# Moving the second layer's modulation out of the prelude and onto GpSimd, inside the first three delta heads

## The chip, the cores and the metric

The kernel runs on one core of one Trainium2 chip. The metric is device time in microseconds (us) for one execution, as the median of several runs. In the profile the engines are called PE (TensorE), DVE (VectorE), ACT (ScalarE), POOL (GpSimd) and SP (SyncE, which only issues DMAs here). SBUF is the on-chip memory that all engines reach, PSUM the one in which TensorE adds up.

## The reference

Two blocks run one behind the other on 256 tokens (the first also on 256 context tokens), all in float32. The part that matters here is the first block: two layers, each of which begins with a modulation, a shift, a scale and a gate per channel, worked out from one conditioning vector for the latent tokens and one for the context.

```python
sc_lat, sc_ctx = jax.nn.silu(c), jax.nn.silu(c_ctx)
for i in range(DEPTH):                     # DEPTH = 2
    shift, scale, gate = jnp.split(sc_lat @ ada_w[i] + ada_b[i], 3, axis=-1)
    shift_c, scale_c, gate_c = jnp.split(sc_ctx @ ada_w[i] + ada_b[i], 3, axis=-1)
    u_lat = rms_norm(h_lat, norm_g[i]) * (1.0 + scale[:, None]) + shift[:, None]
    u_ctx = rms_norm(h_ctx, norm_g[i]) * (1.0 + scale_c) + shift_c
    ...     # layer 0: gated delta rule, 8 key heads; layer 1: attention
```

ada_w[i] is 1024 x 3072 float32, 12.6 MB for each layer. The second layer's modulation depends on c and c_ctx alone, and nothing needs it before the first layer has ended.

## The kernel before

The kernel is a row of stages. In each stage every engine has its own list of instructions, and semaphores tie them together; `Chain` (`link` in the code) makes an engine wait for each of its own instructions before the next. Weights come through a ring, `w_ring`: two sets of slots of 512 KB, filled by SP in groups (`Stream.in_stage`). SP fills a set when TensorE has used what lay in it.

The **prelude** is the first stage. It runs over 12 groups of four weight chunks, six for each layer. For a group, TensorE multiplies the two columns silu(c) with 512 columns of weights (`row_sums`, L505), VectorE copies the sums to SBUF (`row_out`, L588), TensorE turns them so that channels lie on partitions (`turn`, L517), and VectorE adds the bias (`add`, L593). The first layer's six groups are mixed with the norm of h and the gates of the delta rule, whose last pieces are exponentials on ScalarE (L578 to L580) and copies into `sc` on VectorE (`put`, L485). Four of the second layer's groups come after them.

Then a short stage clears two buffers on GpSimd (L752, L753) while VectorE casts and copies some constants (L760 to L763). A stage with the front of head 0 follows, and then one long stage with **eight heads** (`QK_HEADS`, numbered from 0). In head n, TensorE inverts the triangular matrices by levels and then goes through four scan steps. Between these it runs the projections of head n+1 in small portions (`front.products`, L798). VectorE does the masks, differences and states of head n, and between them the convolution of head n+1: one `conv` is L824 and four times L826, and after it comes a `silu`, L832. In step 1 of the scan it does one conv, in steps 2 and 3 one silu and one conv each. At the end of a head GpSimd takes two inverse roots (`inverse_root`, L148: first `rc` for head n+1's norms, then `ms` for head n's output) and scales the output, L1000. TensorE spreads `rc` over partitions (L162), and VectorE scales q and k by it (L860), convolves the last part and builds the next head's matrices (L905). What has to come after what on an engine is the order of the code; there is no scheduler.

SP waits, before it loads the ring's next group of six chunks, until the first head's six projections are done (`summed`, once per head).

Of the kernel before, what the change touches and what calls it, by code (L numbers as in the profile page):

```python
# [21 lines left out]
P = 128  # L22
D = 1024
KT = D // P
# [141 lines left out]
class Sets:  # L166
# [3 lines left out]
    SIZE = 56  # L170
# [296 lines left out]
def prelude(nc, st, bank, C, h, h_loaded, c_cols, g_cols, biases, mods, rows, pick, silu_c, sq, rs, gs, u, w_ab, dt_rows, a_rows, sc,  # L467
# [6 lines left out]
    count, per_layer = 12, 6  # L474
    streams = ((0, CTX, 1), (CTX, SEQ, 0))
    mod = mods[0]
# [13 lines left out]
    with stage(nc, names) as (s, block):  # L490
# [7 lines left out]
        def _(pe):  # L498
# [45 lines left out]
            row_sums(6)  # L544
# [38 lines left out]
        def _(dve):  # L583
# [6 lines left out]
            def add(g):  # L590
                layer, at = g // per_layer, 4 * (g % per_layer)
                dve.wait_ge(s["turned"], g + 1)
                link(nc.vector.tensor_tensor(mods[layer][:, at:at + 4, :], bank[2 + g % 2][:, 0:8].rearrange("p (j c) -> p j c", c=2),  # L593
                                             biases[layer][:, at:at + 4].unsqueeze(2).to_broadcast([P, 4, 2]), ALU.add), s["added"])
# [51 lines left out]
            row_out(6)  # L646
# [10 lines left out]
            row_out(7)  # L657
            add(6)
# [17 lines left out]
def delta_heads(nc, st, bank, banks, C, CS, u, sc, conv_cols, o_cols, gated, spare):  # L676
# [8 lines left out]
    with ExitStack() as es:  # L685
# [49 lines left out]
        short = es.enter_context(nc.sbuf_tensor("short", [P, 3 * P], mybir.dt.bfloat16))  # L735
        th = y
# [176 lines left out]
        with stage(nc, front_names) as (s, block):  # L913
# [46 lines left out]
            def _(dve):  # L960
# [13 lines left out]
                for c in range(4):  # L974
# [5 lines left out]
                 "o_sum o_sqd o_mean o_root o_norm o_turned o_out ")  # L980
        st.begin(DN_GROUP)
        with stage(nc, names + front_names) as (s, block):
            fronts = [Front(s, zs_of[(n + 1) % 2], hs_of[(n + 1) % 2], n) for n in range(QK_HEADS - 1)]
            st.in_stage(QK_HEADS - 1, DN_GROUP, s["proj"], block)
# [7 lines left out]

            def pool_head(pool, link, n):
# [10 lines left out]
            def tensor_head(pe, n):  # L1004
# [145 lines left out]
                if more:  # L1150
# [10 lines left out]
                    ahead(REST)  # L1161
                    pe.wait_ge(s["kq_done"], front.up("kq_done", 2))
# [83 lines left out]
            def vector_head(dve, link, n):  # L1246
# [77 lines left out]
                if more:  # L1324
# [5 lines left out]
                    output(1)  # L1330
                    front.chain(dve, link, 2)
# [300 lines left out]
def flat(a):  # L1632

    return a.rearrange("p a b -> p (a b)")
# [1157 lines left out]
def build(nc, a, out, col_at):  # L2792

    with ExitStack() as top:
# [36 lines left out]
        with ExitStack() as es:  # L2831
# [5 lines left out]
            with ExitStack() as l0:  # L2837
                sc = sb("sc", [P, QK_HEADS, PER_HEAD], l0)
                o_cols = sb("o_cols", [P, 1], l0)
                with ExitStack() as e3:  # L2840
# [5 lines left out]
                    sc_t = sb("silu_c", [P, KT, 2], e3)  # L2846
# [603 lines left out]
```

## Time and profile before

| | us |
|---|---|
| median of 3 runs (2161.9 to 2168.11) | 2164.07 |
| the profiled execution's own time | 2163.62 |
| its span, first to last instruction | 2161.8 |
| TensorE busy in the span | 1962.7 |
| VectorE busy | 1031.1 |
| ScalarE busy | 595.1 |
| GpSimd busy | 74.1 |

The span is shorter than the time by what lies around the instructions. TensorE's busy time is modelled and includes overlaps, so a share near 100% in a stretch means that it hardly waits there. The profile's granted clock is TensorE's, as a share of 2.4 GHz; its mean is 0.955.

### The profile page before, as it was taken

How to read it: one execution, taken by the hardware profiler on the slowest of the kernel's cores; microseconds unless marked ns; L12 is line 12 of the kernel's file. 1: busy time of each engine (PE TensorE's matmuls, PEld its weight loads, DVE VectorE, ACT ScalarE, POOL GpSimd, SP SyncE). 2: the span in 40 equal slices, each digit the busy share in tenths (PEclk: the TensorE clock that was granted, in tenths of full speed). 3: DMA queues.
4: the chain of work that ended last, by engine and by line, in shares of the span. 5: the costliest groups of instructions: out<-in, count | busy, mean ns of one | idle time of the engine just before them, and what ended most of it. 6: DMA issues, size and time to landing. Idle time of an engine off the chain costs nothing. (4 is left out here: it accounts for less than half of the span.)

```text
span 2161.8 us, 40136 instructions
## 1 busy us (share of the span) xinstructions
PE 1962.7 (91%) x16700; PEld 1438.4 (67%) x16700; DVE 1031.1 (48%) x2064; ACT 595.1 (28%) x1275; POOL 74.1 (3%) x50
## 2 busy tenths in 40 slices
PE   5789999999999999789798889988989899989998
PEld 2346666666666666544376777767776798878887
DVE  3346756675766767411114457775455543311101
ACT  1023434444343434400203324232332321000000
POOL 0000101000010101000000000000000000000000
PEclk8899999999999999889899989989999999999999
DMA  8801001010101010022131243231012122434443
GB/s 326 303 31 61 35 26 60 2 60 1 60 1 61 1 61 1 2 117 78 44 117 40 78 169 117 91 119 46 32 60 89 60 78 79 175 117 156 155 176 136
DMA packets 52240, 184.73 MB, mean 85 GB/s; under 512 B 5856, under 2 KB 9312, under 8 KB 51552
## 3 DMA queue, kind: packets, MB, share of 16 engines
q1 hardware_dynamic: 52064, 182.23, 22.5%
q8 instruction: 130, 2.13, 0.4%
q14 instruction: 46, 0.38, 0.1%
HBM read 180.11 MB, written 2.10 MB: 84 GB/s over the span
## 5 line engine op out<-in xcount | busy, mean ns | idle before, releaser
L798 PE MATMUL banks<-u,w_ring 128*128 128x512 f32 x768 | 356.7, 600 | 6.4 <-PEq L195 6.4
L386 PE MATMUL banks<-u,w_ring 128*128 128x256 f32 x1056 | 251.4, 390 | 8.4 <-PEq L195 8.4
L798 PEld LDWEIGHTS banks<-u,w_ring 128*128 128x128 f32 x768 | 140.5, 192 | 133.2 <-issue 130.1
L386 PEld LDWEIGHTS banks<-u,w_ring 128*128 128x128 f32 x1056 | 200.1, 196 | 42.6 <-issue 17.4
L410 PE MATMUL banks<-u,w_ring 128*128 128x256 f32 x704 | 153.7, 382 | 4.8 <-PEq L195 4.8
L410 PEld LDWEIGHTS banks<-u,w_ring 128*128 128x128 f32 x704 | 134.8, 192 | 23.6 <-issue 5.0
L3229 PE MATMUL banks<-gated,w_ring 128*128 128x512 f32 (+1 forms) x384 | 140.9, 530 | 2.8 <-PEq L195 2.8
L3229 PEld LDWEIGHTS banks<-gated,w_ring 128*128 128x128 f32 x384 | 73.9, 193 | 69.4 <-issue 66.2
L826 DVE SCALAR_TENSOR_TENSOR acc<-raw,hc,acc 128x512 f32<-128x512 f32 x128 | 96.2, 752 | 4.5
L3229 PE MATMUL banks<-ffn,w_ring 128*128 128x256 f32 x352 | 77.9, 385 | 3.0 <-PEq L195 3.0
L1195 ACT ACTIVATE acc<-banks 128x512 f32<-128x512 f32 x80 | 47.8, 597 | 105.4 <-PE banks L1060 105.2
L3229 PEld LDWEIGHTS banks<-ffn,w_ring 128*128 128x128 f32 x352 | 68.0, 194 | 12.8 <-issue 3.4
L3084 DVE SCALAR_TENSOR_TENSOR ffn_tanh<-ffn_tanh,banks 128x256 f32<-128x256 f32 x22 | 9.2, 417 | 136.7 <-ACT ffn_tanh L3076 136.7
L1272 DVE TENSOR_TENSOR y<-banks,const_base 128x512 f32<-128x512 f32 x80 | 55.3, 691 | 34.8 <-PE banks L1049 33.6
L1049 PE MATMUL banks<-acc,a_t 64*64 64x64 f32 x2560 | 60.2, 232 | 11.9 <-issue 7.4
L1276 DVE TENSOR_TENSOR acc<-acc,banks 128x512 f32<-128x512 f32 x80 | 55.1, 688 | 33.2 <-PE banks L1076 31.6
L441 PE MATMUL banks<-u,w_ring 128*128 128x256 f32 (+1 forms) x192 | 57.5, 462 | 12.8 <-PEq L195 12.8
L1076 PE MATMUL banks<-y,acc 64*64 64x64 f32 x2560 | 57.9, 228 | 12.2 <-ACT acc L1195 5.5
L3123 ACT ACTIVATE tail_sq<-h 128x256 f32<-128x256 f32 (+1 forms) x28 | 13.2, 470 | 194.3 <-DVE h L2871 91.7
L1049 PEld LDWEIGHTS banks<-acc,a_t 64*64 64x64 f32 x2560 | 48.4, 141 | 25.3 <-issue 16.2
L1076 PEld LDWEIGHTS banks<-y,acc 64*64 64x64 f32 x2560 | 47.5, 137 | 24.4 <-issue 19.3
L1218 ACT ACTIVATE dec<-banks,hs 128x128 f32<-128x128 f32 x128 | 47.1, 368 | 57.2 <-PE banks L1133 53.8
(490 smaller groups left out, 3141.9 us busy)
## 6 DMA issues: line engine op xcount, KB each, us to landing
w_ring<-in_w SPq DMA_DIRECT2D x321, 512.0 KB, 6.2
h<-in_h SPq DMA_DIRECT2D x2, 2048.0 KB, 10.0
const_base<-in_const SPq DMA_DIRECT2D x1, 1216.0 KB, 5.5
hold<-h SPq DMA_DIRECT2D x1, 1024.0 KB, 5.5
const_part<-in_const SPq DMA_DIRECT2D x1, 1024.0 KB, 4.9
h<-hold SPq DMA_DIRECT2D x1, 1024.0 KB, 9.4
out<-u SPq DMA_DIRECT2D x8, 128.0 KB, 1.9
const_part<-in_const SPq DMA_DIRECT2D x1, 640.0 KB, 4.5
```

The costliest lines, as they stand in the source:

```text
L386: mm = self.nc.tensor.matmul(place, self.st.chunk(g % 2, slot)[:, P * k:P * k + P], self.src(k), start=(k == 0), stop=(k == KT - 1))
L410: last = nc.tensor.matmul(out, lhs[k], rhs[k], start=(k == 0), stop=(k == n - 1))
L441: mm = nc.tensor.matmul(bank[q % banks][:, 0:n_tok], st.chunk(h, c)[:, P * b:P * b + P], src(k), start=(k == 0), stop=(k == k_tiles - 1))
L798: mm = nc.tensor.matmul(self.places[m % len(self.places)][:, :], (st.slot(m) if g is None else st.chunk(g % 2, m))[:, P * k:P * k + P], u[ ...
L826: link(nc.vector.scalar_tensor_tensor(out, raw[:, m, :, i:i + SEQ], hc[:, 5 * m + i:5 * m + i + 1], out, ALU.mult, ALU.add), self.s["conv" ...
L1049: mm = nc.tensor.matmul(block_of(bank[2 * d + hb], t, j), a_block(2 * j + d, t, hb, hb), inv[half(hb), d, 2 * t + j, :], start=True, stop= ...
L1076: mm = nc.tensor.matmul(block_of(bank[2 * d + j], t, hb), invt_c[half(j), d, 2 * t + hb, :], prod[half(j), d, hb, t, :], start=True, stop= ...
L1195: link(nc.scalar.activation(invt_c[:, d].rearrange("p s e -> p (s e)"), bank[4 + d][:, :], ACT.Copy), s["t_out"])
L1218: link(nc.scalar.activation(tile(vn[:, d, :], j), tile(bank[2], 2 * d + j), ACT.Copy, scale=col(BETA, 2 * j + d, t)), s["vn_ready"] if j a ...
L1272: link(nc.vector.tensor_tensor(prod[:, d], both(sums(2 * d, 256)), mask(d, lv), ALU.mult), s["p_ready"])
L1276: link(nc.vector.tensor_tensor(by_chain(inv[:, d]), by_chain(inv[:, d]), both(sums(2 * d, 256)), ALU.subtract), s["t_ready"])
L3229: mm = nc.tensor.matmul(bank[m % banks][:, 0:n], st.chunk(g % 2, c)[:, P * (at % 8):P * (at % 8) + P], src(k), start=(k == 0), stop=(k == ...
```

## The change

The second layer's six groups go out of the prelude: 24 chunks less in the ring, six fewer `row_sums`, `row_out`, `turn` and `add`. The same weights are now an input of their own (`mods`, 24 chunks of 128 x 1024). SP loads them in heads 0, 1 and 2, eight for each head, behind the ring's group of that head, into two buffers in `gated` (whose slots for later heads are still free). GpSimd multiplies each chunk with silu(c), once for each of the two streams, and adds the products up in four accumulators (`modulation`), ahead of the two roots of that head. TensorE sums the accumulators over the partitions with 16 one-column products (`modulation_sums`), and VectorE adds the bias (`modulation_out`). The code, cut to its core:

```diff
-def prelude(nc, st, bank, C, h, h_loaded, c_cols, g_cols, biases, mods, rows, pick, silu_c, sq, rs, gs, u, w_ab, dt_rows, a_rows, sc,
+def prelude(nc, st, bank, C, h, h_loaded, c_cols, g_cols, bias, mod, rows, pick, silu_c, sq, rs, gs, u, w_ab, dt_rows, a_rows, sc,
-    count, per_layer = 12, 6
+    count = 6
...
             row_sums(5)
             turn(4)
-            row_sums(6)
             turn(5)
...
             nc.tensor.matmul(bank[4][:, 0:P], C("ones"), lg, start=True, stop=True).then_inc(s["sums"], 1)
-            for g in range(7, count):
-                row_sums(g)
-                turn(g - 1)
-            turn(count - 1)
...
             link(nc.vector.tensor_tensor(gx, lg, bank[4][:, 0:128], ALU.add), s["ex"])
-            row_out(7)
-            add(6)
             dve.wait_ge(s["e_ready"], 4)
...
-            for g in range(8, count):
-                row_out(g)
-                add(g - 1)
-            add(count - 1)
...
+        MOD_HEADS, MOD_CHUNKS = 3, 8
+        w_of = [flat(gated[:, 6 + 2 * i:8 + 2 * i, :]) for i in range(2)]
+        w_part = flat(gated[:, 10:12, :])
+        mod_acc = [[gated[:, 12 + 2 * i + c, :] for c in range(2)] for i in range(2)]
...
+            def mods_in(sp, n, lo, hi):
+                for i in range(lo, hi):
+                    q = MOD_CHUNKS * n + i
+                    if q >= 2:
+                        sp.wait_ge(s["w_used"], q - 1)
+                    sp.dma_start(w_of[q % 2], mod_w[q]).then_inc(s["w_in_odd" if q % 2 else "w_in_even"], 16)
...
-            st.in_stage(QK_HEADS - 1, DN_GROUP, s["proj"], block)
+            st.in_stage(QK_HEADS - 1, DN_GROUP, s["proj"], block, None, {n: all_in(n) for n in range(MOD_HEADS)})
...
+            def modulation(pool, link, n):
+                if n:
+                    pool.wait_ge(s["mod_summed"], n)
+                for i in range(MOD_CHUNKS):
+                    q, at = MOD_CHUNKS * n + i, 2 * (i % 4)
+                    w = w_of[q % 2].rearrange("p (j e) -> p j e", j=2)
+                    pool.wait_ge(s["w_in_odd" if q % 2 else "w_in_even"], 16 * (q // 2) + 16)
+                    for c in range(2):
+                        out = mod_acc[i // 4][c]
+                        link(nc.gpsimd.tensor_tensor(w_part.rearrange("p (j e) -> p j e", j=2), w,
+                                                     silu_c[:, at:at + 2, c:c + 1].to_broadcast([P, 2, 512]), ALU.mult),
+                             s["w_used"] if c else None)
+                        if at:
+                            link(nc.gpsimd.tensor_tensor(out, out, w_part[:, 0:512], ALU.add))
+                        link(nc.gpsimd.tensor_tensor(out, out if at else w_part[:, 0:512], w_part[:, 512:1024], ALU.add),
+                             s["mod_added"] if c and i == MOD_CHUNKS - 1 else None)
...
+            def modulation_sums(pe, n):
+                pe.wait_ge(s["mod_added"], n + 1)
+                for i in range(2):
+                    for c in range(2):
+                        for j in range(4):
+                            col = 8 + 8 * i + 2 * j + c
+                            mm = nc.tensor.matmul(bank[2][:, col:col + 1], tile(mod_acc[i][c], j), C("ones")[:, 0:1],
+                                                  start=True, stop=True)
+                mm.then_inc(s["mod_summed"], 1)
...
             def pool_head(pool, link, n):
...
+                if n < MOD_HEADS:
+                    modulation(pool, link, n)
                 if more:
                     front.root(pool)
...
                     front.grams(pe)
                     ahead(REST)
+                    if n < MOD_HEADS:
+                        modulation_sums(pe, n)
...
                     output(1)
+                    if n < MOD_HEADS:
+                        modulation_out(dve, link, n)
```

What it moves on SP, in the stage with the eight heads (`w_ring<-in_w` is a chunk of the ring, `gated<-in_mods` one of the second layer's modulation):

```order
 L297 UNCONDITIONAL_BRANCH
-L215 DMA w_ring<-in_w 128x1024 x36
+L215 DMA w_ring<-in_w 128x1024 x6
+L986 DMA gated<-in_mods 128x1024 x8
+L215 DMA w_ring<-in_w 128x1024 x6
+L986 DMA gated<-in_mods 128x1024 x8
+L215 DMA w_ring<-in_w 128x1024 x6
+L986 DMA gated<-in_mods 128x1024 x8
+L215 DMA w_ring<-in_w 128x1024 x18
```

Eight loads now stand behind the ring's group of heads 0, 1 and 2 each; each of them but the first two waits until a buffer is free.

On GpSimd, from the start of head 0 in the same stage, before the change (`rc` and `ms` are the two roots, `h` the scaling):

```order
L148 TENSOR_TENSOR rc<-rc,const_base 128x8
L148 TENSOR_TENSOR ms<-ms,const_base 128x8
L1000 TENSOR_TENSOR h<-h,ms 128x1024
L148 TENSOR_TENSOR rc<-rc,const_base 128x8
L148 TENSOR_TENSOR ms<-ms,const_base 128x8
```

and the last pieces of head 0's modulation with what follows, in the changed kernel (L1008 is the product of a chunk, L1012 and L1013 the additions):

```order
L1008 TENSOR_TENSOR gated<-gated,silu_c 128x1024
L1012 TENSOR_TENSOR gated<-gated 128x512
L1013 TENSOR_TENSOR gated<-gated 128x512
L148 TENSOR_TENSOR rc<-rc,const_base 128x8
L148 TENSOR_TENSOR ms<-ms,const_base 128x8
L1040 TENSOR_TENSOR h<-h,ms 128x1024
L1008 TENSOR_TENSOR gated<-gated,silu_c 128x1024
L1013 TENSOR_TENSOR gated<-gated 128x512
```

In heads 0 to 2, 16 products and 28 additions now stand ahead of the roots of the head on this engine.

On TensorE, at the end of head 0 of the changed kernel, from the second of the two Gram products (L866) to the turning of the output (L1210):

```order
L866 MATMUL banks<-qn,kn 128x128 x4
L794 MATMUL banks<-u,w_ring 128x512 x2
L1022 MATMUL banks<-const_base,gated 128x1 x16
L1210 MATMUL banks<-const_base,h 128x128 x8
L881 MATMUL banks<-short 128x512
```

The 16 one-column products, L1022, are new; the rest stood there in this order.

## Rows read from the trace of the kernel before

**Rows 1.** Busy time by stretch, head 1: length, then each engine's busy us.
```profile
core 0: us, PE busy (x) PEld busy (x) DVE busy (x) ACT busy (x) POOL busy (x), PEclk, DMA share, GB/s
...
258.00:355.00 97.00, 93.58 (x1116) 63.48 (x1115) 65.03 (x115) 41.30 (x91) 6.14 (x3) 1.00 0.09 34
```

**Rows 2.** Timeline, the prelude's end: start, duration, engine, line, [idle before].
```profile
69.79 0.28 ACT L580 ACTIVATE gate_tmp<-banks 128x128 f32<-128x128 f32 x1
...
70.53 0.96 DVE L485 COPY sc<-gate_tmp 128x64 f32<-128x64 f32 x4
...
72.12 0.97 DVE L485 COPY sc<-gate_tmp 128x64 f32<-128x64 f32 x4
...
92.81 0.17 DVE L593 TENSOR_TENSOR mod<-banks,cols 128x8 f32<-128x8 f32 x1 [0.77 <-PE banks L517]
```

**Rows 3.** Timeline, the short stage behind the prelude.
```profile
93.54 1.83 POOL L752 MEMSET raw<- 128x2080 f32 x1 [62.45 <-POOLq L195]
93.58 1.87 DVE L760 CAST short<-const_base 128x128 bf16<-128x128 f32 x1 [0.60 <-DVE mod L593]
95.31 1.88 POOL L753 MEMSET inv_t<- 128x2048 f32 x1
95.48 2.05 DVE L760 CAST short<-const_first 128x128 bf16<-128x128 f32 x2
```

**Rows 4.** Timeline, the end of head 1, GpSimd and VectorE.
```profile
337.71 1.23 DVE L1318 TENSOR_TENSOR h<-h 128x1024 f32<-128x1024 f32 x1
337.82 2.61 POOL L148 TENSOR_TENSOR rc<-rc,const_base 128x8 f32<-128x8 f32 x1 [89.70 <-DVE rc L846]
...
341.76 1.63 POOL L148 TENSOR_TENSOR ms<-ms,const_base 128x8 f32<-128x8 f32 x1 [1.33 <-DVE ms L1323]
...
343.47 1.90 POOL L1000 TENSOR_TENSOR h<-h,ms 128x1024 f32<-128x1024 f32 x1
...
343.57 0.69 DVE L860 SCALAR_TENSOR_TENSOR qn<-y,banks 128x512 f32<-128x512 f32 x1
...
344.29 1.36 DVE L824 TENSOR_SCALAR acc<-raw,hc 128x512 f32<-128x512 f32 x1
```

**Rows 5.** Timeline of VectorE in head 1, the scan.
```profile
293.42 0.69 DVE L1284 TENSOR_TENSOR h<-gram_kq,rn 128x512 f32<-128x512 f32 x1
...
298.23 0.43 DVE L1308 COPY state<-banks 128x256 f32<-128x256 f32 x1 [2.39 <-PE banks L1146]
...
304.68 0.49 DVE L824 TENSOR_SCALAR acc<-raw,hc 128x512 f32<-128x512 f32 x1
305.20 3.11 DVE L826 SCALAR_TENSOR_TENSOR acc<-raw,hc,acc 128x512 f32<-128x512 f32 x4
310.47 0.73 DVE L1312 SCALAR_TENSOR_TENSOR state<-state,hs,banks 128x128 f32<-128x128 f32 x2 [2.16 <-PE banks L1146]
...
312.46 0.42 DVE L1315 TENSOR_TENSOR h<-banks,rn 128x256 f32<-128x256 f32 x1
...
322.71 0.73 DVE L1312 SCALAR_TENSOR_TENSOR state<-state,hs,banks 128x128 f32<-128x128 f32 x2 [1.45 <-PE banks L1146]
...
335.36 0.88 DVE L1315 TENSOR_TENSOR h<-banks,rn 128x256 f32<-128x256 f32 x2 [1.85 <-PE banks L1143]
337.51 0.17 DVE L846 TENSOR_SCALAR rc<-banks 128x8 f32<-128x8 f32 x1 [1.26 <-PE banks L155]
```

**Rows 6.** Timeline of TensorE in head 1, three places.
```profile
314.66 0.59 PE L1123 MATMUL banks<-state,kn 128*128 128x256 f32 x2
...
335.55 1.84 PE L155 MATMUL banks<-const_base,gram_kq 128*128 128x1 f32 x16
...
342.13 1.04 PE L162 MATMUL banks<-const_base,rc 128*128 128x128 f32 x8
```

**Rows 7.** Timeline of SP's DMA queue, the groups loaded in heads 0 and 1.
```profile
162.04 2.72 SPq L215 DMA_DIRECT2D w_ring<-in_w  x6
...
263.51 2.80 SPq L215 DMA_DIRECT2D w_ring<-in_w  x6
```

**Rows 8.** DMA issues from 93 to 300 us: size, median us from issue to landing.
```profile
w_ring<-in_w SPq DMA_DIRECT2D x20, 512.0 KB, 7.1
```

More of the change, by code:

```diff
@@ L166 @@
 class Sets:
-    SIZE = 56
+    SIZE = 60
     FIRST = 116
@@ L590, in add @@
             def add(g):
-                layer, at = g // per_layer, 4 * (g % per_layer)
+                at = 4 * g
                 dve.wait_ge(s["turned"], g + 1)
-                link(nc.vector.tensor_tensor(mods[layer][:, at:at + 4, :], bank[2 + g % 2][:, 0:8].rearrange("p (j c) -> p j c", c=2),
-                                             biases[layer][:, at:at + 4].unsqueeze(2).to_broadcast([P, 4, 2]), ALU.add), s["added"])
+                link(nc.vector.tensor_tensor(mod[:, at:at + 4, :], bank[2 + g % 2][:, 0:8].rearrange("p (j c) -> p j c", c=2),
+                                             bias[:, at:at + 4].unsqueeze(2).to_broadcast([P, 4, 2]), ALU.add), s["added"])
             for n in range(2):
@@ L667, in _, with delta_heads @@
                 link(put(BEND, x, d))
-            for g in range(8, count):
-                row_out(g)
-                add(g - 1)
-            add(count - 1)
     st.passed(count, 4)
-def delta_heads(nc, st, bank, banks, C, CS, u, sc, conv_cols, o_cols, gated, spare):
+def delta_heads(nc, st, bank, banks, C, CS, u, sc, conv_cols, o_cols, gated, spare, nxt):
     order = ((0, 1, 2, 3), (1, 0, 3, 2))
@@ L991, in head, with modulation_out @@
                         fronts[n - 1] if n else None, lambda name, count: COUNTS[name] * n + count)
+            def modulation(pool, link, n):
[23 more added lines that the diff above has]
+                mm.then_inc(s["mod_summed"], 1)
+            def modulation_out(dve, link, n):
+                dve.wait_ge(s["mod_summed"], n + 1)
+                link(nc.vector.tensor_tensor(mod_next[:, 8 * n:8 * n + 8, :], bank[2][:, 8:24].rearrange("p (j c) -> p j c", c=2),
+                                             mod_bias[:, 8 * n:8 * n + 8].unsqueeze(2).to_broadcast([P, 8, 2]), ALU.add))
             def pool_head(pool, link, n):
@@ L2854, in build @@
                     finish_loads(nc, loads, small)
-                    prelude(nc, st, bank, C, h, late, cc("c"), cc("norm_g", 0, 8), [cc("ada_b", 24 * i, 24 * i + 24) for i in range(2)],
-                            mods, rows, pick, sc_t, sq, rs, gs, u, w_ab, gate_rows[:, 0, :], gate_rows[:, 1, :], sc, tmp,
+                    prelude(nc, st, bank, C, h, late, cc("c"), cc("norm_g", 0, 8), cc("ada_b", 0, 24),
+                            mods[0], rows, pick, sc_t, sq, rs, gs, u, w_ab, gate_rows[:, 0, :], gate_rows[:, 1, :], sc, tmp,
                             cc("dn_o"), o_cols[:, :])
@@ L2859, in build @@
                 mod = mods[0]
-                delta_heads(nc, st, bank, banks, C, CS, u, sc, cc("conv"), o_cols[:, 0:1], gated, h)
+                delta_heads(nc, st, bank, banks, C, CS, u, sc, cc("conv"), o_cols[:, 0:1], gated, h, (a["mods"], sc_t, mods[1], cc("ada_b", 24, 48)))
                 start_loads(nc, [(h[:, :, :], a["h"].rearrange("p (k t) -> p k t", k=KT))], late)
@@ L3371, in layout @@
     att = f("att_w_in")[0]
-    stream = [row_chunks(ada[0]), row_chunks(ada[1]), fm(np.concatenate(heads, axis=1)), fm_tiles(f("dn_w_out")[0]),
+    stream = [row_chunks(ada[0]), fm(np.concatenate(heads, axis=1)), fm_tiles(f("dn_w_out")[0]),
               fm(att[:, 1024:1536]), fm(att[:, 0:1024]), fm(att[:, 1536:2560]), fm(f("att_w_out")[0])]
```

10 lines of the change are left out of this document (6 added, 4 removed).

## Prediction

> **What bounds the kernel now.** I read the stretches first, then the two places that the change touches. In a head TensorE is busy for 93.58 of 97 us at full clock and VectorE for 65 [rows 1]: the heads run at TensorE's pace, and VectorE has gaps that depend on where in the head it is. The timeline of the prelude's end shows something else. ScalarE's last exponential ends at 70.07, VectorE's last copies into `sc` at 73.09, and then 20 us pass with nothing but the second layer's modulation, up to 92.98 [rows 2]. The next stage waits for that end and begins at 93.54 [rows 3].
>
> **What goes.** Without `row_out(7)` and `add(6)` ahead of them the copies start at 70.1 instead of 70.53, so the prelude ends at about 92.98 - 20.3 = 72.7: **20.3 us less**. The row before, `row_out(6)`, lay in a wait and gives nothing. The ring holds head 0's first chunks by then, since SP ordered them when group 4 was summed. What follows moves as a block. Bounds: 19 and 21.
>
> **GpSimd's work.** Nearest row for a product: L1000, 128 x 1024 with a broadcast input, 1.90 us; the gap between linked instructions is 0.08 (341.76 + 1.63 to 343.47) [rows 4]. No row shows a 128 x 512 addition on GpSimd; half of L1000 is 0.95, the whole of it 1.90, and I take 0.98, since the form is the same and only the fixed part isn't halved. A head: 16 x 1.90 + 28 x 0.98 + 44 x 0.08 = **61.3 us**, mean instruction 1.31. The chunks come behind six of the ring: SP issues those from 263.51 to 266.31 in head 1 [rows 7], and a chunk lands 7.1 us after its issue [rows 8], so GpSimd starts at about 274 (in this trace's time) and, alone, ends at 335.3. Behind it on GpSimd waits `rc`'s root, wanted at 337.8 [rows 4]. In head 0 it starts at about 172.5, some 4 us earlier in the head.
>
> **Do the two engines hinder each other?** The rows say so. VectorE's first cast started at 93.58, took 1.87 and ended 0.08 behind GpSimd's memset; the next one got in only behind the second memset [rows 3]. So an instruction waits for the whole of the other's, and they take turns. The same at the end of a head: L824 takes 0.49 alone, but beside L1000 it took 1.36 and ended 0.28 behind it [rows 4, 5]. The root takes 1.63 alone and 2.61 beside L1318, which reads two SBUF tensors [rows 4]. L860, with one SBUF tensor and one in PSUM, took 0.69 beside L1000, as without it [rows 4]. What no row shows is a VectorE instruction with two SBUF tensors, L826, held up by a long GpSimd instruction. Its price lies between 0 and a whole GpSimd instruction. I take the turns of [rows 3], because L1318 shows that this kind uses what GpSimd needs.
>
> The Trainium skill (SBUF — State Buffer, Who interferes with whom) has this as a rule: "A DVE instruction with two SBUF inputs contends with a GpSimd instruction that reads SBUF", and the one that starts second is blocked until the other is done. By it the sum below stands at 2165; by the rows of casts and L824 alone, only L824 and small copies would pay, and the sum would be 2147.
>
> **The cost in a head.** Of an instruction of VectorE 0.49 - 0.27 = 0.22 us is hidden behind the other's [rows 4, 5], so a turn costs 1.31 - 0.22 = 1.09, the first of a run half an instruction, 0.7.
> - L1284, two small copies and L1299: 4.0 us more. VectorE waits 2.39 for TensorE right behind them [rows 5], and TensorE reaches the result about as much later. Nothing.
> - Step 1, a conv: 0.7 + 4 x 1.09 = 5.1. Cover: VectorE's wait of 2.16, and TensorE takes the state at 314.66 although it is there at 312.88, 1.78 [rows 5, 6]. Left: 1.1.
> - Step 2, silu and conv: 6.1, cover 1.45 + 1.78. Left: 2.9.
> - Step 3: 6.1, cover 1.85 + 1.26 [rows 5]. Left: 3.0.
>
> So `rc`'s mean (L846) is 7.0 late, at 344.5. GpSimd is itself held up by some 20 instructions for 0.45 each or less, about 8 us, and ends at 335.3 + 8 = 343.4: just ahead of it, so the root isn't late for GpSimd's sake. The spread on TensorE had 1.7 to spare (340.43 to 342.13), but `ms` and L1000 are 7.0 late and hold up the last conv: **6.6** a head. In head 0 the modulation ends 4 us earlier, and step 3 pays a third: **4.7**. Together 4.7 + 6.6 + 6.6 = **17.9 us**.
>
> **The small parts.** 16 one-column products took 1.84 us [rows 6]. They stand where VectorE is full; turning the output, and with it ScalarE's last decays, comes later, by about 1.2 us a head: **3.5** with VectorE's addition (0.17 each), bounds 0 and 5.5. The cover is TensorE's lead there; if it is gone, 5.5. The moved DMAs, 24 of 512 KB, fall into a stretch where the engines of the DMA are 9% busy [rows 1]; SP blocks on them until GpSimd is nearly through, but its next group is wanted only a head later.
>
> **Sum**: 2163.62 - 20.3 + 17.9 + 3.5 = 2164.7, say **2165**. The profiled time lies within 0.5 us of the median, so it stands for both.
>
> **Rivals.**
> 1. *No hold-up for two SBUF tensors* (20%). For it: no row shows it. Against: L1318 and the root. Then 2163.6 - 20.3 + 3.5 = 2147.
> 2. *Hold-up at half the price* (12%): VectorE gets two instructions in per turn, or the covers are larger. Runs of 3 and 3.5 instead of 5.1 and 6.1 stay within their covers, only the last leaves some: some 2 us a head, 2153. Faster too.
> 3. *GpSimd becomes the bound* (25%). The margin to the root is 344.5 - 343.4, 1.1 us. If an addition takes 1.15 instead of 0.98, a head's modulation is 4.8 us longer; the root starts 3.7 later in heads 1 and 2, and every turn costs 0.11 more, over 17 turns 1.9. That is 4 to 6 a head, 2165 + 13 = 2178. It decides from a mean instruction of 1.34. Slower than before.
> 4. *One SBUF tensor is enough* (5%): L1293, L1312 and L1315, some 25 a head, pay as well: 20 us a head, 2220. Against: L860.
>
> The Trainium skill (GPSIMD Engine Reference, Elementwise — side-by-side cycle accounting) bears on rival 3: it gives 4497 ns for a 2048-element addition, an estimate of 1.12 us for 512 and 2.25 for 1024. L1000's 1.90 is lower than that, and the row decides for the product; with 1.12 for the additions alone the estimate would be about 2176.
>
> **How the numbers follow.** My forecast has 38%; its own range, with the bounds of the small parts and of the covers, is 2158 to 2171. 0.3% (6.5 us) is about what a measurement tells from no change. Faster: rivals 1 and 2, 0.32. Same: the forecast, 0.38. Slower: rivals 3 and 4, 0.30. The range goes from 2146, rival 1, to 2181, rival 3; it leaves out the lower part of 1, the upper part of 3, and 4.
>
> **What would show it.** Right: the prelude's last VectorE instruction at about 72.7; L1008 at 1.9 us and L1012 at 0.98; in heads 0 to 2 the four L826 of a conv spread over 8 us instead of 3.1, each ending about 0.6 behind a GpSimd instruction; levels ahead of the scan unchanged; heads 3 to 6 unchanged; three heads longer by 6 to 8 us. If L826 stays at 0.75 in the first three heads, rival 1 holds. If the root starts right behind L1013 and long after L846, it is rival 3. If L1315 or L1293 are stretched, it is rival 4. Wrong from the start would be a prelude that ends later than 74, or a first product of head 0 that waits for its chunk.

## The result, and the profile after

The changed kernel takes 2197.53 us (median of 4 runs, 2193.54 to 2207.41), the kernel before 2165.63 us (median of 4, 2161.9 to 2168.11). The ratio is 1.0169, 95% interval 1.0148 to 1.0191: 32 us slower, where "no change" was forecast with 2146 to 2181 as the range. The profiled execution is the one of 2207.41 us, span 2205.7; its prelude ran at a lower clock than that of most other kernels below, and I come back to it.

The timeline of the prelude in the changed kernel, and where the next stage begins [rows 3]:

```profile
50.14 13.92 PE L538 MATMUL banks<-w_ab,u 128*128 128x64 f32 x64
...
83.50 1.83 POOL L748 MEMSET raw<- 128x2080 f32 x1 [51.74 <-POOLq L195]
```

The memset that stood at 93.54 stands at 83.50: 10 us earlier, not 20. The 64 products of L538 take 13.92 us; the line is L539 in the kernel before. The granted clock of this stretch is half:

```profile
50.00:64.00 14.00, 14.00 (x69) 13.74 (x70) 0.69 (x1) 1.37 (x3) 0.00 (x0) 0.50 0.55 218
```

The columns are those of [rows 1]; the third number from the end is the clock, 0.50, that is 1.2 GHz. Now GpSimd in head 1 (start, duration, engine), with SP's queue above it:

```profile
271.57 2.79 SPq L215 DMA_DIRECT2D w_ring<-in_w  x6
274.40 62.09 SPq L986 DMA_DIRECT2D gated<-in_mods  x8
```

```profile
284.18 1.89 POOL L1008 TENSOR_TENSOR gated<-gated,silu_c 128x1024 f32<-128x1024 f32 x1 [34.84 <-DMA gated<-in_mods]
286.15 1.27 POOL L1013 TENSOR_TENSOR gated<-gated 128x512 f32<-128x512 f32 x1
...
355.97 2.22 POOL L1008 TENSOR_TENSOR gated<-gated,silu_c 128x1024 f32<-128x1024 f32 x1
...
359.61 1.26 POOL L1013 TENSOR_TENSOR gated<-gated 128x512 f32<-128x512 f32 x1
360.95 1.65 POOL L148 TENSOR_TENSOR rc<-rc,const_base 128x8 f32<-128x8 f32 x1
```

A product takes the 1.89 us that were expected. An addition takes 1.27, not 0.98. A head's modulation lasts from 284.18 to 360.87, 76.7 us, and `rc`'s root starts right behind it. VectorE in the same head, the scan [rows 5] and what follows:

```profile
310.43 1.51 DVE L1335 SCALAR_TENSOR_TENSOR rn<-banks,hs,v_t 128x128 f32<-128x128 f32 x4 [2.23 <-PE banks L1163]
311.98 1.08 DVE L820 TENSOR_SCALAR acc<-raw,hc 128x512 f32<-128x512 f32 x1
313.09 7.28 DVE L822 SCALAR_TENSOR_TENSOR acc<-raw,hc,acc 128x512 f32<-128x512 f32 x4
...
325.23 2.10 DVE L828 SCALAR_TENSOR_TENSOR y<-y,acc 128x512 f32<-128x512 f32 x1
327.37 1.38 DVE L820 TENSOR_SCALAR acc<-raw,hc 128x512 f32<-128x512 f32 x1
328.78 7.91 DVE L822 SCALAR_TENSOR_TENSOR acc<-raw,hc,acc 128x512 f32<-128x512 f32 x4
...
344.47 7.92 DVE L822 SCALAR_TENSOR_TENSOR acc<-raw,hc,acc 128x512 f32<-128x512 f32 x4
...
353.34 0.17 DVE L842 TENSOR_SCALAR rc<-banks 128x8 f32<-128x8 f32 x1
...
363.94 0.69 DVE L856 SCALAR_TENSOR_TENSOR kn<-y,banks 128x512 f32<-128x512 f32 x1 [5.72 <-PE banks L162]
...
376.22 0.75 DVE L1295 SCALAR_TENSOR_TENSOR gated<-banks,o_cols,zs 128x512 f32<-128x512 f32 x1 [4.96 <-PE banks L1210]
```

The four L822 of a conv (L826 before) take 7.3 to 7.9 us instead of 3.11, while L1335, with one SBUF tensor, still takes 1.51 for four. The mean (L842) starts at 353.34 and the root at 360.95, 7.6 us behind it, where it was 0.3 before [rows 4, 5]: the root waits for GpSimd. Then VectorE waits twice, 5.72 us for the spread of the root and 4.96 for the turned output. TensorE in that place:

```profile
362.74 1.94 PE L162 MATMUL banks<-const_base,rc 128*128 128x128 f32 x8 [6.35 <-POOL rc L148]
...
370.99 4.17 PE L1022 MATMUL banks<-const_base,gated 128*128 128x1 f32 x32
375.02 1.95 PE L1210 MATMUL banks<-const_base,h 128*128 128x128 f32 x8
...
377.19 1.92 PE L885 MATMUL banks<-const_base,hs 128*128 128x128 f32 x8
```

Three things are to be seen: it stood idle for the root, its spread then took 1.94 where it took 1.04 [rows 6], and the sixteen sums are 32 instructions and 4.17 us. (The `order` view ahead of the prediction lists the program's products, x16; a trace lists instructions, x32.)

Since the prelude's clock differs from execution to execution, I compare the heads by a length that leaves it out: from the start of `rc`'s root in the stage ahead of head 0 to that of head 5, read from GpSimd's timeline. It is 128.9 to 734.6 before and 119.9 to 778.7 after: 605.7 and 658.8 us. So heads 0 to 5 lost 53.0 us in this execution and the prelude gave 9.0 back; the spans differ by 43.9, so on balance nothing is to be explained behind the heads. The experiments are given with this length too, as "the heads".

Each head can be cut in three, at the starts of the root, of the scan's first L1335 and of `rc`'s mean: what lies behind the root of the head before, with the levels; the scan; and the wait of the root, from the mean to the root. Before, the scan takes 34.4 us and the wait 0.2 to 0.3 in each of the six heads. The last three columns, read from the profiled executions, give the difference to before, summed over heads 0 to 5. The columns of the scan and of the root are steady: kernels in which GpSimd has no modulation work stay within 0.2 of before. The column behind the root is not: the kernel with the modulation left out runs the same heads as the kernel before and differs by 3.6, so a few us there, and in the length of the heads, tell nothing.

| kernel | median us | ratio to before | the heads, us | behind the root | scan | root late |
|---|---|---|---|---|---|---|
| before | 2165.63 | | 605.7 | | | |
| changed | 2197.53 | 1.0169 | 658.8 | 10.9 | 23.0 | 19.1 |
| modulation left out | 2141.88 | 0.9912 | 602.0 | -3.6 | -0.2 | 0.0 |
| sums only | 2154.48 | 0.9963 | 606.7 | 1.0 | -0.1 | 0.0 |
| sums only, in two halves | 2147.94 | 0.9937 | 605.3 | -0.4 | -0.1 | 0.0 |
| write-only GpSimd | 2162.6 | 0.9997 | 619.5 | 2.0 | -0.2 | 11.9 |
| products only, early | 2152.66 | 0.9954 | 613.7 | 7.4 | 0.5 | 0.1 |
| products only, late | 2188.59 | 1.0113 | 649.6 | 9.8 | 34.0 | 0.1 |
| wide additions | 2191.22 | 1.0135 | 652.1 | 9.8 | 36.5 | 0.1 |
| sums later | 2197.06 | 1.0151 | 658.6 | 7.7 | 26.1 | 19.1 |
| five heads | 2171.11 | 1.0036 | 630.1 | 10.1 | 9.7 | 4.5 |
| even chunks | 2160.95 | 0.9998 | 621.8 | 8.1 | 8.0 | 0.1 |
| even and early | 2156.2 | 0.9968 | 614.5 | 4.5 | 4.3 | 0.1 |

Each ratio is to runs of the kernel before on the same chip; their medians are 2165.63 beside the changed kernel and 2161.14 to 2163.15 beside the others.

### The profile page after: what moved, and what is told of

The parts are those of the page before. It is cut to its first block and busy times, and to the rows that moved or that the text cites. A ratio compares the mean times of both kernels' runs of the same rounds, so it can differ in the third digit from the quotient of the medians.

```text
span 2205.7 us, 40172 instructions
## 1 busy us (share of the span) xinstructions
PE 1977.3 (90%) x16652; PEld 1460.1 (66%) x16652; DVE 1090.5 (49%) x2055; ACT 594.5 (27%) x1275; POOL 292.1 (13%) x182
## 5 line engine op out<-in xcount | busy, mean ns | idle before, releaser
L794 PE MATMUL banks<-u,w_ring 128*128 128x512 f32 x768 | 364.3, 611 | 13.3 <-PEq L195 13.3
L822 DVE SCALAR_TENSOR_TENSOR acc<-raw,hc,acc 128x512 f32<-128x512 f32 x128 | 136.3, 1065 | 4.5
L1008 POOL TENSOR_TENSOR gated<-gated,silu_c 128x1024 f32<-128x1024 f32 x48 | 97.4, 2030 | 119.9 <-DMA gated<-in_mods 116.4
L148 POOL TENSOR_TENSOR rc<-rc,const_base 128x8 f32<-128x8 f32 x8 | 17.0, 2126 | 405.0 <-DVE rc L842 404.8
L1013 POOL TENSOR_TENSOR gated<-gated 128x512 f32<-128x512 f32 x48 | 69.9, 1457 | 3.8
L441 PE MATMUL banks<-u,w_ring 128*128 128x256 f32 (+1 forms) x192 | 57.7, 463 | 12.8 <-PEq L195 12.8
```

Of the source, the lines that this page charges most:

```text
L441: mm = nc.tensor.matmul(bank[q % banks][:, 0:n_tok], st.chunk(h, c)[:, P * b:P * b + P], src(k), start=(k == 0), stop=(k == k_tiles - 1))
L794: mm = nc.tensor.matmul(self.places[m % len(self.places)][:, :], (st.slot(m) if g is None else st.chunk(g % 2, m))[:, P * k:P * k + P], u[ ...
L822: link(nc.vector.scalar_tensor_tensor(out, raw[:, m, :, i:i + SEQ], hc[:, 5 * m + i:5 * m + i + 1], out, ALU.mult, ALU.add), self.s["conv" ...
L1008: link(nc.gpsimd.tensor_tensor(w_part.rearrange("p (j e) -> p j e", j=2), w, silu_c[:, at:at + 2, c:c + 1].to_broadcast([P, 2, 512]), ALU. ...
L1013: link(nc.gpsimd.tensor_tensor(out, out if at else w_part[:, 0:512], w_part[:, 512:1024], ALU.add), s["mod_added"] if c and i == MOD_CHUNK ...
```

## The experiments

My theory after the result: the prelude's gain is whole, and the heads lose it through turns with GpSimd (whose price depends on what of VectorE's work they lie beside), through GpSimd's own length, and through the sums. The rivals: that the products' number alone sets the price, that the moved DMAs or GpSimd's mere activity do, or that the prelude gave only 10.

### The modulation left out

No part of the second layer's modulation is computed; the layer takes the first layer's values.

```
-            st.in_stage(..., {n: all_in(n) for n in range(MOD_HEADS)})
+            st.in_stage(...)
...
-                if n < MOD_HEADS:
-                    modulation(pool, link, n)
```

> The second layer's modulation is left out altogether (its values are a copy of the first layer's): no loads, no GpSimd work, no one-column products. What is left of the change is the shorter prelude. Theory A, the prelude's end moves by its idle tail: 20 us less than before, 2144. Theory B, TensorE's clock takes part of it back, since the work ahead of the end no longer keeps it up (in the changed kernel's trace the first stage ended only 10 us earlier, and head 0 began 7 earlier): 7 to 12 us less, 2153 to 2157.

2141.88 us, ratio 0.9912 (0.9886 to 0.9939): 20.7 us less than before, for the 20.3 of the forecast, as theory A had it. Its prelude:

```profile
47.45 7.36 PE L538 MATMUL banks<-w_ab,u 128*128 128x64 f32 x64
...
73.58 1.83 POOL L748 MEMSET raw<- 128x2080 f32 x1 [42.99 <-POOLq L195]
```

The memset is 20.0 earlier than before, with L538 at full clock. So the prelude gives what was forecast. The clock of L538 is at half in three of the thirteen profiled executions: the changed kernel's, that of five heads and that of even and early. In these three L538 starts later (49.28 to 50.14) than in any of the other ten (46.68 to 49.10), and the clock stands at 0.50 over the 3 us from 47 to 50, where the others show 0.67 to 1.00. Why it doesn't rise there was not tested. It costs some 9 us where it happens; the kernel with the sums later, which does the same prelude as the changed one at full clock, has its memset at 73.58 too.

### The sums only

GpSimd clears the accumulators once, TensorE sums those zeros in heads 0 to 2, VectorE adds the bias; the products and additions are left out, and so are the chunks' DMAs.

```
+                nc.gpsimd.memset(flat(gated[:, 12:16, :]), 0.0).then_inc(s["padded"], 1)
...
-                pe.wait_ge(s["mod_added"], n + 1)
...
-                    modulation(pool, link, n)
```

> As the run before, but with TensorE's 16 one-column products and VectorE's addition in heads 0 to 2, on accumulators that are cleared once (the loads and GpSimd's products and additions are left out). Theory A, the sums cost 1.2 us a head, as predicted: 3.5 us over the kernel without them. Theory B, they are 32 instructions of TensorE and take 3.75 us a head where VectorE waits for the output's turning: 8 to 11 us over the kernel without them.

2154.48 us, 0.9963 (0.9946 to 0.998), on theory B's side: 12.6 more than without, with ten runs from 2147.33 to 2157.98. The spans of the two profiled executions differ by 9.3: 3.0 ahead of the heads' length, 4.7 in it and 1.7 behind it. Of the 3.0, 1.6 come from this experiment's own clearing of the accumulators, beside which two casts of VectorE take 3.61 us instead of 2.05; they aren't a cost of the sums. From head 0's root to head 3's, the stretch that holds the sums, it is 303.5 us, and 295.1 with none: 8.4. TensorE's timeline and its granted clock in head 1:

```profile
330.38 3.63 PE L1022 MATMUL banks<-const_base,gated 128*128 128x1 f32 x32
...
335.02 1.91 PE L886 MATMUL banks<-const_base,hs 128*128 128x128 f32 x8
```

```profile
330.00:334.00 4.00, 4.00 (x35) 3.76 (x34) 2.32 (x6) 0.00 (x0) 0.00 (x0) 1.00 0.00 0
335.00:338.00 3.00, 3.00 (x14) 2.82 (x13) 2.69 (x7) 0.89 (x3) 0.00 (x0) 0.50 0.00 0
```

32 one-column instructions in a row, then half clock: eight transposes in 1.91 us that take 1.05 at full. It doesn't always come. In head 0 of the same execution the clock stays full:

```profile
230.92 3.63 PE L1022 MATMUL banks<-const_base,gated 128*128 128x1 f32 x32
...
235.53 1.05 PE L886 MATMUL banks<-const_base,hs 128*128 128x128 f32 x8
```

Over the traces of the changed kernel and the experiments there are 22 such rows of 32; what follows is slowed in 19 and not in 3.

### GpSimd that only writes

Each product and each addition is replaced by a memset of about its duration (the values are not computed). The memsets are a little shorter (1.80 and 1.23 us, against 1.89 and 1.27). The DMAs, their waits and the sums stay.

```
-                        link(nc.gpsimd.tensor_tensor(w_part..., w, silu_c..., ALU.mult), ...)
+                        link(nc.gpsimd.memset(mod_clear[:, 0:2048], 0.0), ...)
...
-                            link(nc.gpsimd.tensor_tensor(out, out, w_part[:, 0:512], ALU.add))
+                            link(nc.gpsimd.memset(mod_clear[:, 0:1360], 0.0))
```

> GpSimd's products and additions are replaced by as many memsets of about the same length (1.88 and 1.27 us), which write SBUF and read nothing; the modulation's values are zero plus bias. The loads, the waits, the order and the sums stay. Theory A (turns with VectorE's two-tensor instructions because GpSimd reads): L822 goes back to 0.75 us; GpSimd still holds the root back by its own length, since 69 us from its start end some 8 us behind the root's time; so the heads are 8 to 10 us longer than before instead of 19, and the kernel about 30 us faster than the changed one. Theory B (any GpSimd instruction holds up any VectorE instruction with two SBUF tensors): L822 stays near 1.8 us and the time stays at 2195.

2162.6 us, 0.9997 (0.9977 to 1.0017): 35 us less than the changed kernel, 39.3 in the heads, and theory A holds. In head 1, GpSimd first, VectorE's convs behind it:

```profile
266.48 1.81 POOL L1007 MEMSET gated<- 128x2048 f32 x1 [34.89 <-DMA gated<-in_mods]
```

```profile
295.24 3.11 DVE L823 SCALAR_TENSOR_TENSOR acc<-raw,hc,acc 128x512 f32<-128x512 f32 x4
...
319.47 1.99 DVE L821 TENSOR_SCALAR acc<-raw,hc 128x512 f32<-128x512 f32 x1
```

L823 is back at 3.11 with GpSimd at work all through the scan, for 66.3 us in this head. This is the largest part of the loss: GpSimd's reading. The Trainium skill (SBUF — State Buffer, Who interferes with whom) says that a VectorE instruction with two SBUF inputs contends with a GpSimd instruction that reads SBUF and not with one that only writes; the trace agrees, 7.28 beside reads and 3.11 beside writes. L821, with one input, took 0.49 alone and 1.99 here: some instructions are held up by writes too. But that costs nothing here: the scan's column is back at that of the kernel before. The heads are still 12.8 longer than with the sums only, and 11.9 of that is the root, which starts 5.8 us behind the mean in head 1. That is the price of GpSimd's length alone.

### Wide additions

Three of four pairs of 128 x 512 additions become one of 128 x 1024: the same elements, fewer and longer instructions.

```
-                            link(nc.gpsimd.tensor_tensor(out, out, w_part[:, 0:512], ALU.add))
-                        link(nc.gpsimd.tensor_tensor(out, ..., w_part[:, 512:1024], ALU.add), ...)
+                            link(nc.gpsimd.tensor_tensor(wide, wide, w_part, ALU.add))
```

> The products are added up over 1024 columns at once and folded to 512 once a group: 12 additions of 1024 and 4 of 512 a head instead of 28 of 512. All of the reference is computed. Alone, GpSimd then needs 61 us a head instead of 70. Theory A (GpSimd's length decides, the root waits for it): 9 us less in each of three heads, 25 us less than the changed kernel, about 2170. Theory B (VectorE's waits in the convolutions decide): each turn is longer, 1.9 us instead of 1.5, so nothing is won or 5 to 10 us lost.

2191.22 us, 1.0135 (1.0107 to 1.0162). GpSimd in heads 1 and 2, and the root of head 1:

```profile
L1014 POOL TENSOR_TENSOR gated<-gated 128x1024 f32<-128x1024 f32 x24 | 60.5, 2522 | 1.9
```

```profile
351.63 2.62 POOL L148 TENSOR_TENSOR rc<-rc,const_base 128x8 f32<-128x8 f32 x1 [4.23 <-DVE rc L843]
```

GpSimd is idle for 4.23 us ahead of the root: it is no longer late. Yet only 6.3 us came back, since each turn is now with a longer instruction: a conv's four L823 take 9.00 and 10.06 us in steps 1 and 2 of head 1, where L822 took 7.28 and 7.91. Against the changed kernel the root gives 19.0 us back and the scan takes 13.5 more. Neither theory has it all: length and turns are two costs, and this edit pays one with the other.

### Products alone, early and late

Two kernels with the sixteen products of a head and no additions (so the modulation's values are not computed). In the first GpSimd starts as the chunk lands; in the second it waits for the first residual of the scan's step 1.

```
+                    if i == 0:
+                        pool.wait_ge(s["r_ready"], COUNTS["r_ready"] * n + 1)
```

> GpSimd makes only the sixteen products of a head, the additions are left out (so the modulation's values are not those of the reference); they begin as the chunks land, near 284 us in head 1, and last 16 x 1.97 = 32 us, so that they end near the scan's step 1. Theory A (turns cost by what of the scan they lie beside): only step 1 meets some, 2154 plus about 1 to 3 us a head, 2155 to 2163. Theory B (a product costs VectorE the same anywhere): the turns' whole share stays, some 30 us over the kernel with the sums alone, near 2185.

> The same products alone, but GpSimd waits in each head until the scan's step 1 has its triangle ready, so that they lie beside steps 1 to 3 of the scan (some 304 to 342 us in head 1) with no addition between them. Theory A (turns cost by what they lie beside, and a stall by how much of GpSimd's time the products take): one conversion of four pieces loses up to 7 us, three steps some 15 us a head, 45 us over the run with the sums alone: 2200, between 2185 and 2210. Theory B (as many products, the same price): the same time as with the early products.

Early: 2152.66 us, 0.9954 (0.9936 to 0.9972). Late: 2188.59, 1.0113 (1.0076 to 1.015). The same products and DMAs, 36 us apart in the medians and 36.0 in the heads. GpSimd and VectorE in head 1, early:

```profile
259.20 33.27 POOL L1008 TENSOR_TENSOR gated<-gated,silu_c 128x1024 f32<-128x1024 f32 x16 [31.50 <-DMA gated<-in_mods]
```

```profile
288.45 6.14 DVE L823 SCALAR_TENSOR_TENSOR acc<-raw,hc,acc 128x512 f32<-128x512 f32 x4
...
300.70 3.11 DVE L823 SCALAR_TENSOR_TENSOR acc<-raw,hc,acc 128x512 f32<-128x512 f32 x4
```

and late:

```profile
299.18 34.54 POOL L1010 TENSOR_TENSOR gated<-gated,silu_c 128x1024 f32<-128x1024 f32 x16 [60.23 <-DVE rn L1334]
```

```profile
301.39 9.16 DVE L823 SCALAR_TENSOR_TENSOR acc<-raw,hc,acc 128x512 f32<-128x512 f32 x4
...
318.86 9.16 DVE L823 SCALAR_TENSOR_TENSOR acc<-raw,hc,acc 128x512 f32<-128x512 f32 x4
...
335.13 3.12 DVE L823 SCALAR_TENSOR_TENSOR acc<-raw,hc,acc 128x512 f32<-128x512 f32 x4
```

Late, two convs have 9.16 us; early, one has 6.14, and the head hardly notices (100.2 us from root to root, 99.5 with the sums only). It takes 112.6 with the late ones. In both the root starts right behind the mean, so GpSimd's length plays no part; the scan's column is 0.5 early and 34.0 late. So a product has no price of its own: beside the levels it costs the scan nothing, and the first stretched conv is covered. The early kernel also carries all 24 chunks. It is not slower than the sums only by the medians; its heads are 7.0 longer, 1.0 of it between head 0's root and head 3's and the rest where the column behind the root wanders, so a cost of the moved DMAs of a few us is neither shown nor ruled out. The late kernel is 34.1 us over the sums only, 11.4 a head, which is what the scan's column shows; some 15 were expected, from three stretched convs, and in head 1 two were.

### The sums later

TensorE's sums go behind the turning of the output.

```
-                    if n < MOD_HEADS:
-                        modulation_sums(pe, n)
                     pe.wait_ge(s["kq_done"], front.up("kq_done", 2))
...
                     front.rows(pe, 3)
+                    if n < MOD_HEADS:
+                        modulation_sums(pe, n)
```

> The changed kernel with TensorE's sixteen column sums of a head put behind the turning of the output's four tiles instead of ahead of it. Nothing is left out. Theory A (the sums stand on the path that VectorE waits for at the output, 3.75 us a head): 2 to 3.5 us a head come back, 2187 to 2191. Theory B (the 12.6 us that the kernel with the sums alone lost come from something else, the clock or the extra output row): no more than 2 us, 2195 to 2199.

2197.06 us, 1.0151 (1.0118 to 1.0185): nothing came back, and theory A of this run is wrong. TensorE in head 1:

```profile
363.14 1.05 PE L885 MATMUL banks<-const_base,hs 128*128 128x128 f32 x8
364.03 3.94 PE L1022 MATMUL banks<-const_base,gated 128*128 128x1 f32 x32
367.83 6.75 PE L794 MATMUL banks<-u,w_ring 128*128 128x512 f32 x8
```

```profile
367.80:374.00 6.20, 6.20 (x9) 2.58 (x10) 5.07 (x12) 0.49 (x1) 0.00 (x0) 0.50 0.00 0
```

The output is turned in time now, but the clock is at 0.50 behind the sums here too, and eight wide products take 6.75 us instead of 3.60. The sums are more than their 3.6 us on one path: in most heads they bring the half clock to whatever stands behind them.

### The sums in two halves

The kernel with the sums only, with four of TensorE's wide products between two halves.

```
+                        modulation_sums(pe, n, 0)
                     ahead(REST)
-                        modulation_sums(pe, n)
+                        modulation_sums(pe, n, 1)
```

> The kernel with the sums alone (TensorE sums zeros, GpSimd does none of the modulation, so its values are not those of the reference), its 32 one-column products a head in two halves with four of TensorE's wide products between. Theory A (32 in a row are little work for TensorE, the granted clock falls to half behind them, and that is most of what the sums cost): the clock stays full, L794 behind them at 0.43 us a product and L885 at 1.05 for eight, 2 to 3.5 us a head less than 2154.5: near 2146. Theory B (only the 3.6 us that they take count): 2154, as before.

2147.94 us, 0.9937 (0.9915 to 0.9958), 6.5 less than with the sums in a row. From head 0's root to head 3's it is 299.7 us here, 303.5 with the sums in a row and 295.1 with none, so 3.8 of the 6.5 are seen in the trace. (The table's length shows only 1.4, since the part of it ahead of head 0's root, where no sums stand, was 2.7 longer in this execution.) Both kernels clear the accumulators.

```profile
333.74 1.84 PE L1021 MATMUL banks<-const_base,gated 128*128 128x1 f32 x16
335.45 1.96 PE L795 MATMUL banks<-u,w_ring 128*128 128x512 f32 x4
337.25 1.84 PE L1021 MATMUL banks<-const_base,gated 128*128 128x1 f32 x16
...
340.07 1.05 PE L886 MATMUL banks<-const_base,hs 128*128 128x128 f32 x8
```

The clock stays full: L886 takes 1.05, and so it does in heads 0 and 2. In the four kernels with groups of 16 (this one and the three below) all 22 such groups are followed by work at full clock.

### Five heads, even chunks, and an early start

Three kernels that compute everything. The first spreads the six groups of four chunks as 2, 1, 1, 1, 1 over heads 0 to 4; the second as 6, 5, 5, 4, 4 chunks, with the sums of the head that completes two groups in two halves; the third also fetches the next head's first two chunks early and lets GpSimd begin with the levels.

```
-        MOD_HEADS, MOD_CHUNKS = 3, 8
+        MOD_HEADS, GROUPS, FIRST_GROUP = 5, (2, 1, 1, 1, 1), (0, 2, 3, 4, 5, 6)
```

```
+        MOD_HEADS, CHUNKS_BY, LOADS_BY = 5, (0, 6, 11, 16, 20, 24), (0, 6, 11, 16, 20, 24)
```

```
-        MOD_HEADS, CHUNKS_BY, LOADS_BY = 5, (0, 6, 11, 16, 20, 24), (0, 6, 11, 16, 20, 24)
+        MOD_HEADS, CHUNKS_BY, LOADS_BY = 5, (0, 6, 11, 16, 20, 24), (0, 8, 13, 18, 22, 24)
...
+                    pool.wait_ge(s["t_ready"], COUNTS["t_ready"] * n + 1)
```

> The same 24 chunks, products and additions, spread over five heads: eight in head 0 and four in each of heads 1 to 4. Nothing is left out. Theory A (what costs time is that GpSimd's 77 us run past the point where the mean waits for the root, and that the turns fall in steps 2 and 3 of the scan): four chunks take some 33 to 38 us, begin near 284 us after the span's start and end near the scan's step 1, so no root comes late in heads 1 to 4, and steps 2 and 3 have no product beside them; against the changed kernel -8 for the length and some two thirds of the turns of heads 1 and 2, but two more heads have sums of 1.2 to 4 us: 2174, between 2168 and 2182. Theory B (each instruction of VectorE that meets a product pays the same wherever it stands, so the number of products alone sets the price): same number of products, 2190 to 2200.

> The same 24 chunks over five heads, but 6, 5, 5, 4 and 4 of them instead of 8, 4, 4, 4 and 4, the accumulators carried from head to head; the one head that completes two groups sums them in two parts, with four of TensorE's wide products between. Nothing is left out. Theory A (what costs is GpSimd working past the scan's step 1, the root held up, and TensorE's clock halved by 32 one-column products in a row): the five-heads kernel lost 5.2 us in head 0 to the late root, some 7 to the clock and some 5 to turns late in head 0's scan; two thirds of that come back, heads 1 and 2 pay some 1 us more each: 2159, between 2154 and 2166. Theory B (the number of chunks and sums sets the price): 2171, as the five-heads kernel.

> As the kernel with even chunks, but SyncE fetches the next head's first two chunks at the end of this head's, and GpSimd begins in heads 1 to 4 when the first matrix of the levels is ready, some 12 us earlier, beside VectorE instructions that read at most one SBUF tensor. Nothing is left out. Theory A (turns cost by what they lie beside): four heads get back the turns in front of and in the scan's step 1, some 1 to 2 us each: 4 to 8 us below the kernel with even chunks, near 2153. Theory B (a product costs the same anywhere): the same time as that kernel.

Five heads: 2171.11 us, 1.0036 (1.0016 to 1.0056), 26 less than the changed kernel with the same products, additions and sums. Even chunks: 2160.95, 0.9998 (0.9982 to 1.0015). Even and early: 2156.2, 0.9968 (0.9954 to 0.9982), the only full version that is faster than the kernel before. The last two change more than one thing each (even chunks the spread and the sums, the last one also the loads and the start), so the shares of these aren't parted by the medians; the table's columns show which part of a head gave. Head 2 with five heads, GpSimd and then VectorE:

```profile
417.29 1.60 POOL L1013 TENSOR_TENSOR gated<-gated 128x512 f32<-128x512 f32 x1
446.11 2.62 POOL L148 TENSOR_TENSOR rc<-rc,const_base 128x8 f32<-128x8 f32 x1 [27.22 <-DVE rc L842]
```

```profile
413.83 6.40 DVE L822 SCALAR_TENSOR_TENSOR acc<-raw,hc,acc 128x512 f32<-128x512 f32 x4
...
426.46 3.12 DVE L822 SCALAR_TENSOR_TENSOR acc<-raw,hc,acc 128x512 f32<-128x512 f32 x4
```

GpSimd is through in step 1 of the scan and idles for 27 us ahead of the root. The 4.5 us of late root and 7.4 of the 9.7 in the scan fall in head 0, which still has eight chunks; with even chunks the root is late nowhere. From one root to the next it is 100.6 to 101.7 us in heads 2 to 4, where it is 118.0 in head 2 of the changed kernel. In the last version GpSimd starts 17 us after its output scaling in head 1, where it was 35 in the changed kernel:

```profile
259.83 1.89 POOL L1009 TENSOR_TENSOR gated<-gated,silu_c 128x1024 f32<-128x1024 f32 x1 [16.97 <-DVE acc L1317]
```

14 us still separate it from the kernel without the modulation, 12.5 of them in the heads.

## Why the prediction was wrong

**"20.3 us less" in the prelude** was right: 20.7 by the medians with the modulation left out, whose last VectorE instruction of the prelude ends at 73.0 (72.7 forecast). In the changed kernel's profiled execution the prelude ended 10 us later, so the sign "later than 74" was there, but through the clock of L538.

**The forecast for the heads, term by term**, against the table:

| | forecast | measured |
|---|---|---|
| turns in the scan | 17.9 (4.7, 6.6, 6.6) | 23.0 (7.4, 8.5, 7.2) |
| root late for GpSimd's sake | 0 | 19.1 (4.5, 7.3, 7.3) |
| sums, and what stands behind the root | 3.5 | 10.9 |
| together | 21.4 | 53.0 |

**The step that failed is that GpSimd ends "just ahead of it, so the root isn't late for GpSimd's sake"**, and under it "I take 0.98". The addition takes 1.27 (halving the one neighbouring row took a product with a broadcast factor for an addition of two full tensors), which is 8 us a head. The prediction itself named the point, a mean instruction of 1.34; unhindered it is (16 x 1.89 + 28 x 1.27) / 44 = 1.50, so rival 3 came to pass, and at a higher price than it had. In head 1 GpSimd began 40.2 us behind the root of the head before (284.18 - 244.00) instead of 33.5, since SP reached the chunks later and the first landed 9.8 us after its issue instead of 7.1 [rows 8]; and its work took 76.7 us instead of 69.4. Together 14.0 us, against a margin of 1.1 and a mean that itself came 5.3 later than forecast (109.3 behind the last root instead of 104.0): 7.6 are left, for 3.7 in the rival. By these numbers, as an estimate and with the mean where it was, the late start or the longer additions alone would have made the root about 1 us late or less; it took both.

**Who hinders whom** was right: L822 at 7.28 rules out rival 1, L1335 unchanged rival 4, and the write-only kernel shows that it is the reading. **The price of a turn** came out near the forecast, 1.09, partly by luck: the rows give (7.28 - 3.11) / 4 = 1.04 in step 1 and 1.20 in steps 2 and 3, but the forecast's own rule, the mean instruction less 0.22, would give 1.28 with the mean that was measured. In steps 1 to 3 VectorE fell back by 1.0, 4.1 and 3.4 us against the start of step 1 (1.1, 2.9 and 3.0 forecast), 8.5 for 7.0. Ahead of step 1, the row from L1326 to L1341 took 3.2 us more (4.0 forecast) and cost nothing, as forecast, and the levels' instructions kept their 0.69 us. Heads 3 to 6 were not all unchanged: head 3 is 3.4 us longer, all of it behind the root of head 2.

**"16 one-column products took 1.84"** misread [rows 6]. Its x16 is instructions; a float32 product of this kind is two of them (`rc` has eight columns, for x16), so 16 products are x32 and 3.6 to 4.2 us. What stands behind mostly runs at half clock, which the forecast had nowhere; and the root's lateness brings the same through another door: TensorE idles 6.35 us and its spread runs at half.

**By the experiments**, the 56.8 us between the heads of the changed kernel and of the one without the modulation (658.8 - 602.0) are: sums 4.7; GpSimd busy without reading 12.8, nearly all of it the late root; its reading 39.3. Of these 39.3, 23 are turns in the scan and 7 the root, later still since GpSimd's instructions are held up and since the memsets were some 3 us a head shorter; 9 lie behind the roots. The column behind the root wanders by some 4 us, so the split of 4.7 and 9 is rough.

**What stays open:** the prelude's clock in some executions; why the clock stayed full behind 3 of the 22 rows of 32; and how the 10.9 us behind the roots divide between the sums, the half clock and the late spread.

## What to carry to other kernels

Work for an idle engine is priced by the place where it lies, not by its amount: ask what the other engine reads in that stretch, and what waits in the queue behind the new work. Where a forecast hangs on a margin of 1 us under 60 us of work whose main instruction no row shows, give the rival more than the forecast. A change that loses as a whole may win when it is spread thinner, here over five heads and into the stretches with at most one SBUF tensor an instruction.

## What the runs showed of the hardware that was not expected

- 32 one-column instructions in a row were followed by slowed work in 19 of 22 cases (1.53 to 1.92 us for eight transposes that take 1.05, 5.17 to 6.75 for eight wide products that take 3.60), with a granted clock of 0.50 in the stretches read, although TensorE was busy for 4.00 of 4.00 us ahead of it; 16, four wide ones (1.96 us) and 16 again left it at 1.00, as did 16 alone.
- A float32 128 x 512 addition on GpSimd takes 1.27 us, a 128 x 1024 product with a broadcast factor 1.89, a 128 x 1024 addition 2.37 (median of 36 with wide additions). So an addition's length goes almost by elements, and a product with a broadcast factor is cheaper than an addition of the same size, which is why half of [rows 4]'s 1.90 was too little. Whether the factor or the operation makes it cheaper no run parts.
- Products of 1.89 us in an unbroken row stretch a VectorE instruction of 0.78 us to 2.29 (9.16 / 4), products and additions mixed to 1.82 to 1.98: VectorE gets in once for each of GpSimd's. Products that were held up themselves take 2.22 us, and with the gap of 0.08 that is the 2.29 of the pair.
- GpSimd's memsets, which read nothing, left L823 at 3.11 but held L821 up to 1.99, which cost the scan nothing (34.4 us, as before).
